# A hybrid encoder step in float32: the mixer's input projections in pairs, as seven block products in place of eight, with the values first

## What is computed

```python
def mixer(xn, conv_prev, gla_prev, w_in, w_alpha, b_alpha, conv_w, g_conv, g_gla, w_out):
    z = xn @ w_in
    bg, cg, h, q, k, v, gr, r = jnp.split(z, SPLITS, axis=-1)
    cv, conv_new = causal_dwconv(cg * h, conv_prev, conv_w)
    y_conv = rmsnorm(bg * cv, g_conv)
    logg = jax.nn.log_sigmoid((gr @ w_alpha + b_alpha).astype(jnp.float32)) / GATE_TAU
    ...
    o, gla_new = gla(q, k, v, logg, gla_prev)
    o = rmsnorm(o, g_gla).astype(xn.dtype).reshape(Bsz, L, D_GLA)
    y_gla = o * jax.nn.silu(r)
    y = jnp.concatenate([y_conv, y_gla], axis=-1) @ w_out
    return y, conv_new, gla_new

def conv_ffn(xn, prev, w_up, conv_w, w_down):
    u = xn @ w_up
    uc, new = causal_dwconv(u, prev, conv_w)
    a, g = jnp.split(uc, 2, axis=-1)
    return (jax.nn.silu(g) * a) @ w_down, new
```

## Time and profile before

| | us |
|---|---|
| median of three runs | 2422.65 (2420.15 to 2423.34) |
| the profiled execution, its own time | 2420.94 |
| its span in the profile | 2419.2 |
| PE busy | 2320.1 (96%) |
| DVE busy | 1586.5 (66%) |
| ACT busy | 975.5 (40%) |
| POOL busy | 1142.3 (47%) |

### The profile page before, as it was taken

One profiled execution on the slowest core, in us unless ns is written; L12 is line 12 of the kernel. 1 busy time (PEld: TensorE's weight loads), 2 busy tenths in 40 slices (PEclk: granted clock), 3 DMA queues, 4 the chain that ended last, 5 costly groups with the idle time before them and its releaser, 6 DMA issues. The chain is left out here.

```text
span 2419.2 us, 38967 instructions
## 1 busy us (share of the span) xinstructions
PE 2320.1 (96%) x12962; PEld 2113.1 (87%) x12962; DVE 1586.5 (66%) x2397; ACT 975.5 (40%) x1881; POOL 1142.3 (47%) x1117
## 2 busy tenths in 40 slices
PE   7999999999999999799999998999999988999997
PEld 6889878899788987799999998899999987999996
DVE  2046662155650656698988988667667677878886
ACT  4333353333353435444444445333333335444443
POOL 3222323222423334778878785444444445455552
PEclk9999999999999999899999999999999999999999
DMA  5111335111452234744444457644444456555553
GB/s 158 59 53 44 122 114 172 50 44 42 151 183 78 79 120 147 272 170 150 162 173 147 165 175 258 206 160 144 141 160 150 139 183 231 196 191 191 186 195 106
DMA packets 257550, 355.01 MB, mean 147 GB/s; under 512 B 12189, under 2 KB 195314, under 8 KB 257458
## 3 DMA queue, kind: packets, MB, share of 16 engines
q1 hardware_dynamic: 257457, 353.77, 43.8%
HBM read 276.54 MB, written 77.19 MB: 146 GB/s over the span
## 5 line engine op out<-in xcount | busy, mean ns | idle before, releaser
L1434 PE MATMUL ps<-xo,wq 128*128 128x384 f32 (+1 forms) x1848 | 599.7, 324 | 27.6 <-issue 12.0
L1435 PE MATMUL ps<-xo,wq 128*128 128x384 f32 (+1 forms) x1848 | 598.6, 324 | 0.0
L1436 PE MATMUL ps<-xo,wq 128*128 128x384 f32 (+1 forms) x1848 | 598.0, 324 | 0.0
L2089 DVE TENSOR_TENSOR resid<-resid,ps 128x512 f32<-128x512 f32 (+1 forms) x728 | 477.2, 680 | 76.1 <-PE ps L1436 45.3
L485 POOL TENSOR_TENSOR w_lo<-raw,w_hi 128x512 fp32r<-128x512 f32 x192 | 251.4, 1337 | 566.5 <-ACT w_hi L478 566.5
L906 POOL TENSOR_TENSOR wq<-wu_raw,wq 128x256 fp32r<-128x256 f32 x396 | 378.2, 978 | 118.2 <-ACT wq L1018 118.2
L1434 PEld LDWEIGHTS ps<-xo,wq 128*128 128x128 f32 x1848 | 350.4, 190 | 50.5 <-issue 28.0
L1435 PEld LDWEIGHTS ps<-xo,wq 128*128 128x128 f32 x1848 | 351.0, 190 | 20.1
L1436 PEld LDWEIGHTS ps<-xo,wq 128*128 128x128 f32 x1848 | 351.3, 190 | 0.0
L1434 PE MATMUL ps<-xt_hi,w_hi 128*128 128x384 f32 (+4 forms) x960 | 316.7, 330 | 7.9 <-DVE xt_lo L1807 3.7
L2106 DVE SCALAR_TENSOR_TENSOR up_y<-up_u,params,up_y 128x768 f32<-128x768 f32 (+1 forms) x264 | 287.3, 1088 | 50.2 <-ACT up_y L1062 31.5
(11 more groups left out here) (207 smaller groups left out, 3499.2 us busy)
## 6 DMA issues: line engine op xcount, KB each, us to landing
wq<-w_ops SPq DMA_DIRECT2D x176, 512.0 KB, 4.4
wu_raw<-in_w_up_dram SPq DMA_DIRECT2D x89, 512.0 KB, 4.1
w_ops<-wq SPq DMA_DIRECT2D x88, 512.0 KB, 2.7
raw<-in_w_in_dram SPq DMA_DIRECT2D x72, 512.0 KB, 3.9
wd_raw<-in_w_down_dram SPq DMA_DIRECT2D x66, 512.0 KB, 5.1
x_in<-in_x_prompt_dram SPq DMA_DIRECT2D x32, 512.0 KB, 4.5
raw<-in_w_out_dram SPq DMA_DIRECT2D x24, 512.0 KB, 3.4
wu_raw<-in_w_up_dram SPq DMA_DIRECT2D x43, 256.0 KB, 3.1
```

Source lines behind the costliest of these rows:

```text
L1434: pe.matmul(out, lh, rh, start=(first and n == 0), stop=False, skip_group_check=skip)
L1435: pe.matmul(out, ll, rh, start=False, stop=False, skip_group_check=skip)
L1436: last = pe.matmul(out, lh, rl, start=False, stop=end, skip_group_check=skip)
L2089: last = dve.tensor_tensor(resid[0:m, t, s], resid[0:m, t, s], ps[0:m, bank, :], ALU.add)
```

## The change

The order of a block's mixer is now: the values (stage v) first, then the gate projection, then ten pairs in place of stage z and of the conv units. A pair (PAIRS) is two units of 128 outputs that were worked singly: r, q with q, k with k, cg, h and bg. Each pair is made by the FFN's scheme of seven block products (pair_product), 84 matmuls of 384 (290) columns where two units took 96. The x operands of the products 1, 3, 4 and 5 are sums of blocks of xt: t_3, t_2 and the sum for product 5 are made by DVE (operand_step, operand_low), t_1 by POOL, their high parts by ACT (high_sum). The sum for product 5 is written over a block of xt_hi and xt_lo, once the values and the gate have been made. The weight operands go through wu_raw, wu_sum and wq as in the FFN: DVE makes S1 to S4 for each pair (pair_sums), ACT the seven high parts (high_pair), and POOL alone the seven low parts, two instructions of 256 columns each (pair_low; LOW_PAIRS and LOW_OPS are empty, so DVE takes none).

The GLA's first tile is prepared within the early pairs (AT_GATE, AT_SUMS, AT_SCORES); its steps X, Y and Z lie between the products from (4, 3) on, and the last five products (LEFT) follow after them. The buffers are placed anew (raw over wu_raw and wu_sum, t_1 and conv_y over tst, t_3 and t_2 over xs_a and xs_b), which adds waits for stores; XO_AT and the order of SP's loads ahead of the FFN are changed, so that the FFN's first operands are loaded and split earlier. The FFN's steps are otherwise as they were. The diff, cut to its core:

```diff
-Z_CHUNKS = [[(0, 256), (256, 512)], [(0, 256), (256, 512)], [(0, 256), (256, 324)]]
...
-BEFORE = {
-    "z": (0, 0, 0, 0), "v": (2, 2, 2, 2),
-    "conv": (3, 3, 3, 3), "out": (7, 7, 7, 3), "end": (9, 9, 9, 5),
-}
+BEFORE = {"v": 0, "out": 1, "end": 3}
+
+RAW_AT = [3, 2, 1, 0]
+
+
+PAIRS = [("r", 0), ("r", 2), ("qk", 0), ("qk", 2)] + [(kind, j) for j in (0, 2) for kind in ("cg", "h", "bg")]
+NPAIR = len(PAIRS)
+
+AT_GATE, AT_SUMS, AT_SCORES = (1, 6), (3, 1), (4, 2)
+
+LEFT = 5
+
+LOW_PAIRS, LOW_OPS = (), ()
 
 FFN_TAP, FFN_PREV, CONV_TAP, CONV_PREV, G_CONV, G_GLA = 0, 3, 5, 8, 10, 11
 NX = 3
-
-T_PRODUCT, T_SUMS, T_SCORES = 0, 2, 4
...
-XO_AT = [1, 3, 4, 0, 2, 5, 6]
+XO_AT = [4, 5, 6, 1, 3, 0, 2]
 
 
...
-                "z_done": ng + nt, "z_read": ng + nt, "zeros": 3, "c_done": 3 * CJ * nch, "cg_read": CJ * nch,
-                "u_done": CJ * nch, "conv_step": 3 * CJ * nch, "y_done": CJ * nch, "pre": nt, "pre_b": nt,
+                "v_done": nt, "v_read": nt, "g_done": nch, "g_read": nch, "zeros": 3,
+                "t_step": 8, "t1_step": 3, "t_hi": 4, "t_lo": 4,
+                "w_loaded0": 16 * NPAIR, "w_loaded1": 16 * NPAIR, "w_summed": 4 * NPAIR, "w_hi": NP * NPAIR,
+                "p_done": NP * NPAIR, "r1_read": NPAIR, "r2_read": NPAIR, "r3_read": NPAIR,
+                "c11_read": NPAIR, "c12_read": NPAIR, "c21_read": NPAIR, "c22_read": NPAIR,
+                "u_done": 2, "y_first": CJ, "conv_step": 2 * CJ, "y_done": 2, "pre": nt, "pre_b": nt,
...
+        def pair_operand(b, i, part):
+
+            c = HALF[b]
+            if i in (1, 3, 4):
+                return {1: t_2, 3: t_3, 4: t_1}[i][:, part, :, 0:c]
+            k, c0 = {0: (0, 0), 2: (4, 0), 5: (0, c), 6: (4, c)}[i]
...
+        def pair_out(b, p, row, half):
+
+            kind, u = PAIRS[p]
+            c = HALF[b]
+            if kind in ("h", "bg"):
+                return conv_u[row][:, 2 + half * c:2 + (half + 1) * c]
+            return {"r": gla_y, "qk": qk, "cg": conv_y}[kind][:, u + row, half * c:(half + 1) * c]
+
+        def pair_low(eng, s, i, sem, parts):
+
+            eng.wait_ge(mix_sems["w_hi"], NP * s + i + 1)
+            at, w = WQ_AT[i], wu_source(i)
+            for n in range(parts):
+                r = slice(n * 512 // parts, (n + 1) * 512 // parts)
+                last = eng.tensor_tensor(wq[:, at, 1, r], w[:, r], wq[:, at, 0, r].bitcast(F32), ALU.subtract)
+            last.then_inc(sem, 1)
+
+        def pair_split(eng, s, i):
+
+            v, p = pair_lows(s, i)
+            if v:
+                eng.wait_ge(pair_low_v, v)
+            eng.wait_ge(pair_low_p, p)
...
         def mix_events(b):
 
-            groups = [(j, m, c) for j in range(CJ) for m in range(3) for c in range(len(CHUNKS[b]))]
+            products = [(p, i) for p in range(NPAIR) for i in range(NP)]
             steps = [(s, t) for t in range(TILES[b]) for s in ("XYZ" if tile_cols(b, t)[1] == P else "XZ")]
-            out, g = [], 0
+            out, g = [], products.index(AT_SCORES) + 1
+            for p, i in products[:g]:
+                out.append(("G", p, i))
+                if (p, i) in (AT_GATE, AT_SUMS, AT_SCORES):
+                    out.append(({AT_GATE: "P", AT_SUMS: "S", AT_SCORES: "C"}[p, i], 0))
+            rest = len(products) - g - LEFT
             for n, step in enumerate(steps):
                 out.append(step)
-                upto = (n + 1) * len(groups) // len(steps)
-                while g < upto:
-                    out.append(("G",) + groups[g])
-                    g += 1
-            return out
+                upto = len(products) - LEFT - rest + (n + 1) * rest // len(steps)
+                out += [("G",) + product for product in products[g:upto]]
+                g = upto
...
+                unit_free(sp, (0, 1), unit_index(b, "v", 0, 0) + 1)
+                for p in range(NPAIR):
+                    for part in range(2):
+                        if p:
+                            pair_split(sp, NPAIR * b + p - 1, (2, 5)[part])
+                        load_pair(b, p, part)
...
+                n1.wait(pool, "lo", 2 * nt)
+                wait(pool, sums_stored, 16 * 4 * b)
+                if b == NB - 1:
+                    pool.wait_ge(gap_zero, 4)
+                c = HALF[b]
+                t1 = unsplit(b, 4)
+                for step, (left, left_part, right, right_part, op) in enumerate([
+                        (xt_hi, c, xt_hi, 0, ALU.subtract), (None, 0, xt_lo, c, ALU.add), (None, 0, xt_lo, 0, ALU.subtract)]):
+                    mix.wait(pool, "t1_step", step)
+                    for k in range(4):
+                        a = left[:, k, left_part:left_part + c].bitcast(F32) if left else t1[:, k]
+                        last = pool.tensor_tensor(t1[:, k], a, right[:, k, right_part:right_part + c].bitcast(F32), op)
+                    mix.inc(last, "t1_step")
+                for p in range(NPAIR):
+                    for i in range(NP):
+                        if not low_by_v(p, i):
...
+                high_pair(NPAIR * b, 0)
+                high_pair(NPAIR * b, 1)
+                for n, (c0, w) in enumerate(CHUNKS[b]):
+                    mix.wait(act, "g_done", n + 1)
+                    mix.inc(act.activation(gate_in[:, c0:c0 + w], ps[0:2 * RANK, (B_GATE, 2)[n], 0:w], ACT.Copy), "g_read")
+                    high_pair(NPAIR * b, 2 + n)
+                high_sum(5)
+                high_pair(NPAIR * b, 4)
...
+                parts = [(0, (0, 1)), (1, (0, 1)), (0, (2, 3)), (1, (2, 3))] + [(n, range(SLOTS)) for n in range(2, nt)]
+                for g, (n, slots) in enumerate(parts):
+                    values(n, slots)
+                    for turn, blk, i in left[g - 1] if 1 <= g <= len(left) else []:
                         turn(blk, i)
...
+                def pair_product(p, i):
+                    s, c = NPAIR * b + p, HALF[b]
+                    bank = {0: 0, 2: 0, 4: 2, 6: 2}.get(i, 1)
+                    pair_split(pe, s, i)
+                    if p == 0 and i in (1, 3, 4, 5):
+                        mix.wait(pe, "t_lo", (1, 3, 4, 5).index(i) + 1)
+
+                    if i == 0:
+                        mix.wait(pe, "c11_read", p)
+                        mix.wait(pe, "v_read", nt)
+                    if i == 1:
+                        mix.wait(pe, "c21_read", p)
+                    if i == 2:
+                        mix.wait(pe, "r1_read", p + 1)
+                    if i == 3:
+                        mix.wait(pe, "r2_read", p + 1)
+                    if i == 4:
+                        mix.wait(pe, "c12_read", p)
+                        mix.wait(pe, "g_read", nch)
+                    if i == 5:
+                        mix.wait(pe, "r3_read", p + 1)
+                    if i == 6:
+                        mix.wait(pe, "c22_read", p + 1)
+                    hi, lo = (pair_operand(b, i, h) for h in range(2))
+                    mix.inc(product(ps[:, bank, 0:c], [
+                        (wq[:, WQ_AT[i], 0, k * P:(k + 1) * P], wq[:, WQ_AT[i], 1, k * P:(k + 1) * P],
+                         hi[:, k], lo[:, k]) for k in range(4)], first=i in (0, 1, 4), skip=True), "p_done")
+                    if b == 0 and (p, i) == (0, 6):
+
+                        pe.wait_ge(rows_ready, 16 * 12)
...
+                operand_step(0, 3, b22, b12[0], ALU.subtract)
+                operand_step(1, 3, t_raw, b22_l, ALU.add)
+                operand_step(2, 3, t_raw, b12[1], ALU.subtract)
+                operand_step(3, 1, t_raw, b11, ALU.add)
+                operand_step(4, 1, t2_raw, b11_l, ALU.add)
+                pair_sums(0)
+                operand_low(1, 1)
+                operand_low(2, 3)
+                operand_low(3, 4)
+                mix.wait(dve, "v_done", nt)
+                mix.wait(dve, "g_done", nch)
+                mix.wait(dve, "t_lo", 3)
+                t2, n4_raw = high_low(1), unsplit(b, 5)
+                operand_step(5, 5, b21, t2[0], ALU.subtract)
+                operand_step(6, 5, n4_raw, b21_l, ALU.add)
+                operand_step(7, 5, n4_raw, t2[1], ALU.subtract)
+                operand_low(4, 5)
...
+                    if i == 3:
+                        mix.wait(dve, "p_done", done)
+                        mix.inc(dve.tensor_tensor(r_3m[:, 0:c], ps[:, 1, 0:c], r_1[:, 0:c], ALU.add), "r3_read")
+                        if p + 1 < NPAIR:
+                            pair_sums(p + 1)
+                        if kind == "bg":
```

858 lines of the change are left out of this document (468 added, 390 removed).

## The result

| | before | changed |
|---|---|---|
| median, us | 2422.53 (4 runs, 2420.15 to 2423.34) | 2476.38 (4 runs, 2475.78 to 2482.5) |
| ratio of the times | | 1.023 (1.0212 to 1.0247) |
| span of the profiled execution, us | 2419.2 | 2473.7 |
| busy PE / DVE / ACT / POOL, us | 2320.1 / 1586.5 / 975.5 / 1142.3 | 2292.7 / 1817.0 / 1046.9 / 1386.6 |
| mean granted clock of PE | 0.992 | 0.977 |

A forecast was written before the change was run, and what follows sets the result against it. The prediction took the mixers to be bound by PE. Its terms, −59 of PE's work against added waits and −10 into the FFN, summed to +21, some 2 less for common cover: 2420.9 + 19 = 2440 us, range 2403 to 2470.

The forecast's parts named there:

- t_1: At the blocks' start, POOL makes t_1 3 to 6 us late: +13 us for three blocks (0 to 18).
- PE's work removed: In the mixers, fewer matmuls: −22 us each in blocks 0 and 1, −14 to −15 in block 2, sum −59.
- GLA phase: From product (4, 3) on, DVE's clumps make PE's GLA steps and products wait: +40 us (lower +12, upper +55).
- start of the pairs (r_1): Product 2 waits for ACT's copy r_1 behind product 5's high part: +18 us in three blocks (14 to 27).
- values first: In blocks 1 and 2 the values wait for POOL's low parts of the last two slots: +8 us (0 to 13).
- weights of block 2's early pairs: In block 2's early pairs, load, sums, high and low parts take 14.6 us against PE's 11.5: +5 us (0 to 10).
- clock, other places: Waits of about 5 us also cost PE clock: +6 us for all such places.
- into the FFN: On the way into the FFN, first operands are loaded and split earlier: −10 us (0 to −14).
- a wait for t_1 shortens the one for r_1: At the blocks' start, the terms' common cover takes some 2 us off the sum.
- C: Rival, chance 0.13: POOL's low parts bound the pairs, 17 to 20 us a pair; +30 to 2470, slower.
- B: Rival, chance 0.25: DVE clumps hide, the GLA phase costs +12, not +40; about 2412 us, 2395 to 2418.
- D: Rival, chance 0.12: gains and waits cancel, each added wait taking half of its value; 2418 to 2428 us.

The follow-up runs named there:

- Kernel 1: Changed kernel with t_1 made by DVE, ahead of the sums of pair 0, in place of POOL: 2453.74 us.
- kernels 2: Changed kernel with ACT's high part for product 5 moved behind its copy into r_1: 2476.15 us.
- 5: Changed kernel with t_1 by DVE, r_1 ahead of product 5's high part, and DVE's addition into r_2 ahead of its low part: 2461.45 us.
- 9: Kernel 5 with each of POOL's low parts of the pairs as one instruction of 512 columns in place of two of 256: 2462.7 us.
- 10: Kernel 9 with DVE's S1 to S4 of pair 1 moved behind its addition of product 4: 2468.73 us.
- kernel 4: Changed kernel with S1 to S4 shortened to one column from pair 5 on, so the computation is changed: 2454.4 us.
- kernel 6: Kernel 5 with S1 to S4 made by POOL from pair 5 on, ahead of the pair's low parts: 2442.83 us.
- 15: Changed kernel with DVE's two taps per channel group shortened to two columns, so the computation is changed: 2463.91 us.
- 14: Changed kernel with POOL's low-part instructions shortened to one column from pair 5 on, so the computation is changed: 2465.49 us.
- kernel 3: Changed kernel with DVE making the low parts of operands 2 and 4 in pairs 1 to 4: 2485.39 us.
- kernel 12: Changed kernel with t_1 by DVE, S1 to S4 from pair 5 on by POOL, and LEFT = 1: 2446.07 us.
- kernel 13: Changed kernel with POOL's low parts from pair 4 on in four instructions of 128 columns: 2474.92 us.

## Why the prediction was wrong

It said slower by 19 us, with 2403 to 2470 as the range; the kernel is slower by 54 and lies above the range. The sign and the kinds of waits were right; one term, t_1, was mis-sized by 17 us, about half of the miss; five others came out 30 us higher together, and two 5 us lower. Term by term, us over the three blocks, measured in the trace of after (and by a run where one is named):

| term | predicted | measured |
|---|---|---|
| PE's work removed | −59 | −59 by the cadence: pairs 1 and 2 take 15.4 and 14.7 us where 84 × 0.174 is 14.6 |
| GLA phase | +40 | +45 |
| start of the pairs (r_1) | +18 | +15 |
| t_1 | +13 | +30 |
| values first | +8 | +8 |
| weights of block 2's early pairs | +5 | +8 |
| clock, other places | +6 | +13 |
| stage out | 0 | +9 |
| into the FFN | −10 | −4 |
| block 0 starts sooner | 0 | −2 |
| sum | +21 | +63, against 54 in the time |

The measured column is read so: the GLA phase is 129.2, 129.7 and 113.0 us against the work of 116, 116 and 91, less the 4 us idle before. r_1 is two waits of 5.5 and the two half-speed products; t_1 is 8.6, 10.0 and 11.6; the clock is the excess of matmuls that started more than 1.5 times their usual distance apart outside a wait, some 35 us up to the FFN against 13 to 18 before (by how the small shapes are counted), less what stands in other rows, so it is the least certain row. The rows overlap, hence 63 and not 54. PE's busy time fell by 27 us and not by the 59 forecast as a sign: slow matmuls count as busy, and some 20 us more of that stand in it.

**The step that failed is t_1.** "Six tiles of values take 33 us, so t_1 comes 3 to 6 us late." It came 9 to 12 us late, because I had it begin behind POOL's low parts for the values, 14 us into a block; "the last stores", which the prediction names beside them, got no time of their own. In block 1 it began 37.5 us in (398.48 against 361.0): it is written over tst, and had to wait for the store of tst. In block 0 it began as soon as xt_lo was complete (39.33), but its instructions of 384 columns took 2.1 us and then 1.9, above the estimate's 1.06 to 1.8, since DVE worked on its own sums without a pause; in block 1, without that, the first four took 0.98 each. Kernel 1 shows that t_1 on POOL is the cause: with t_1 by DVE the three gate stretches fall by 31 us. The start behind the store stays in that kernel and the 16.4 us become 5.3, so start and length together made t_1 late. Kernel 1 also shows a part that I had priced at 2 us for all blocks ("a wait for t_1 shortens the one for r_1"): as long as t_1 holds the start, the chain behind it (gate, three steps of DVE, high part, low part, with r_1, r_2 and an addition queued inside) is half hidden. Freed, it takes 12 us of the 31 back, and kernels 2, 5, 9 and 10 moved its wait from product 2 to 3, to 6 and back to 3 without bringing pair 0 under 20 us, where its matmuls take 14.6 (11.5 in block 2).

**The GLA phase** was read rightly, and its size within 5 us (129.2 and 129.7 against 130; block 2 113 against 105 to 108). DVE bounds it by its clumps, for it is busy 77% of the time: sums 22 us (kernel 4, or 19 in kernel 6), taps 12.5 (15), POOL's turns 11 (14). Two of my sizes inside it were wrong in opposite directions, so that the size came out is in part luck: DVE has 99 us of work in block 0 and not 107. The sums take 0.68 to 0.69 each there, 2.7 a pair and not 4.2, for POOL waits for them and so is silent; and the GLA's own instructions became longer by POOL's low parts (k_end's 418 to 739 ns), for which I had put nothing. These three runs each took one part away, so their sum need not be a split of the 45.

**Weights of block 2's early pairs.** I had PE wait for the cycle of load, sums and POOL's low parts. Its waits there end with DVE's additions instead (1.1 and 2.8 us, and 4.3 at product (0, 6)), which stand in DVE's queue behind S1 to S4, and these behind the load. What else is in the 8 us was not taken apart. **Values first** came to the 8 us of the sum, though its "four runs of twelve matmuls" are two: PE had done 24 when it waited, 7 us into block 1.

**The clock.** I put +6 for all places. The waits of 4.3 to 10 us ahead of the gate's second chunk and in pair 0 have cost 1.4 to 2.4 us each behind them, and in block 2, where waits of 11.6 and 4.3 us follow one another, the granted clock is 0.88 for 68 us. **Stage out** I had left alone. It is 86.3, 85.7 and 67.3 us where it was 84.9, 83.5 and 62.1; PE's waits there for DVE's additions into resid rose from 2.9 to 10.0 us and those for conv_sq from 1.3 to 3.0, and 4.3 us for xt_lo are new. No run took this apart. **Into the FFN**: the wait of 5.0 us for the first operands went, but a wait of 4.3 us for POOL's low part is new and the one for r_1 stayed (4.3 us, 4.2 before), so 4 us came and not 10.

**The rivals.** C came nearest in time (2470) and is wrong in its mechanism: kernel 3 took two of seven low parts from POOL and lost 9 us, and pairs 1 and 2 of block 0 go at or near PE's own cadence. B (a GLA phase of +12) and D are out by the stretches above. POOL matters in the changed kernel less by how long its low parts take than by what they do to DVE and by what stands ahead of them in its queue.

**The shared ports.** The Trainium skill (SBUF — State Buffer, section "Who interferes with whom") calls the port pair that VectorE and GpSimd share an exclusive lock. The rows here agree with that to 0.3 us: beside each other an instruction of DVE (1.76 us alone) and one of POOL (0.72 alone) go by in 2.2 us, where strict turns would take 2.5. I had weighed it for POOL's low parts, and for DVE's side in the sums and taps alone, and not for the GLA's own instructions, which are DVE's as well.

What stays open: a remainder of 24 us over before when t_1 and the late sums are moved (kernel 12). There the stretch from the GLA's first step to stage out is still 11 to 14 us a block over PE's work, and pair 0 takes 24.3 to 25.8 us where its matmuls take 14.6.

## What to carry to other kernels

When a product's operand must be computed first, follow every queue that it stands in, back to the store that frees its buffer, and ask what is queued behind each of its parts: t_1 cost 30 us in PE's waits not by its length alone but because it began behind a store, and the values' last read and all low parts stood behind it. When matmuls are removed from a stage where another engine is at 55% and comes to 77%, price the stage by walking that engine's clumps, not by its busy share. And once a chain of waits is long, moving one link forward moves the wait; measure the next link before counting the gain (kernels 2 and 5).

## What was not expected of the hardware

Where both read two operands from SBUF, VectorE and GpSimd take turns instruction by instruction. Beside an unbroken run of DVE's 1536-column instructions, POOL's 256 columns took 2.2 us and its 512 columns 2.8, against 0.7 and 1.3 alone; DVE's took 2.17 and 2.72, against 1.76 alone (block 1). A long instruction on either side so costs the other one's short ones most, and cutting POOL's into pieces helps DVE and harms POOL (kernel 13: k_end from 739 to 574 ns, POOL's busy time beside the GLA from 66 to 79 us).
